# The 31-tap depthwise convolution of a streaming-encoder trunk: six channel tiles as plain fp32 matmuls on row quarters of TensorE, in place of four tiles as split fp32r on row halves and one on full rows

## The reference

```python
def causal_depthwise_conv(x, w):          # w: 31 taps by 1024 channels
    k, c = w.shape
    return lax.conv_general_dilated(
        x, w[:, None, :].astype(x.dtype), window_strides=(1,), padding=[(k - 1, 0)],
        dimension_numbers=("NWC", "WIO", "NWC"), feature_group_count=c)

def mixer_conformer_conv(x, w_pw1, b_pw1, w_dw, b_dw, ln_g, ln_b, w_pw2):
    h = x @ w_pw1 + b_pw1
    a, g = jnp.split(h, 2, axis=-1)
    h = a * jax.nn.sigmoid(g)
    h = causal_depthwise_conv(h, w_dw) + b_dw
    h = jax.nn.silu(layer_norm(h, ln_g, ln_b))
    return h @ w_pw2
```

## Time and profile before

| | before |
|---|---|
| median of three runs | 2538.86 us (2538.58 to 2539.81) |
| the profiled execution's own time | 2539.48 us |
| span of its trace | 2537.7 us |
| TensorE matmul busy | 2515.6 us, 99% |
| VectorE (DVE) busy | 1955.7 us, 77% |
| ScalarE (ACT) busy | 1201.1 us, 47% |
| DMA | mean 95 GB/s |
| granted TensorE clock | 90% or more of full speed in each of 40 slices |

### The profile page before, as it was taken

How to read it: one execution, slowest core, us unless ns; L and a number is a source line. 1 busy time by engine, 2 the same in 40 slices (tenths; PEclk the granted TensorE clock), 3 DMA queues, 4 the chain that set the end, 5 groups by cost and what they waited for, 6 DMA issues and landing times. The chain is left out here.

```text
span 2537.7 us, 41266 instructions
## 1 busy us (share of the span) xinstructions
PE 2515.6 (99%) x17241; PEld 2312.0 (91%) x17241; DVE 1955.7 (77%) x2571; ACT 1201.1 (47%) x1960; POOL 1.4 (0%) x10
## 2 busy tenths in 40 slices
PE   9999999999999999999999999999999999999999
PEld 7899999889888899998898899998898999999888
DVE  6989999578454679995784479996677979999576
ACT  6766444436233254443362254444356766444335
POOL 0000000000000000000000000000000000000000
PEclk9999999999999999999999999999999999999999
DMA  5203333324232233333233224333222203333322
GB/s 157 74 11 100 108 108 101 108 83 133 92 99 84 84 92 101 108 105 104 83 100 100 92 66 125 101 108 108 92 92 93 67 26 100 101 109 101 108 82 77
DMA packets 267054, 240.10 MB, mean 95 GB/s; under 512 B 14908, under 2 KB 212852, under 8 KB 266740
## 3 DMA queue, kind: packets, MB, share of 16 engines
q1 hardware_dynamic: 266292, 236.94, 30.1%
q10 hardware_dynamic: 576, 0.52, 0.1%
HBM read 233.21 MB, written 2.10 MB: 93 GB/s over the span
## 5 line engine op out<-in xcount | busy, mean ns | idle before, releaser
L1786 DVE TENSOR_TENSOR w_lo<-raw,w_hi 128x1024 fp32r<-128x1024 f32 x287 | 345.2, 1221 | 265.1 <-ACT w_hi L1309 264.6
L1309 ACT CAST w_hi<-raw 128x1024 fp32r<-128x1024 f32 x287 | 294.9, 1046 | 375.2 <-DMA raw<-in_ffn_w_down_dram 106.4
L879 PE MATMUL psum<-h_hi,w_lo 128*128 128x512 f32 x872 | 341.4, 392 | 0.0
L881 PE MATMUL psum<-h_hi,w_hi 128*128 128x512 f32 x872 | 339.3, 389 | 0.0
L880 PE MATMUL psum<-h_lo,w_hi 128*128 128x512 f32 x856 | 333.2, 389 | 0.0
L1024 PE MATMUL psum<-a_hi,w_lo 128*128 128x256 f32 x1088 | 280.0, 285 | 5.2 <-DVE w_lo L1786 3.6
L1024 PE MATMUL psum<-a_hi,w_hi 128*128 128x256 f32 x1088 | 276.6, 283 | 0.0
L1190 PE MATMUL psum<-h_hi,w_hi 128*128 128x256 f32 x768 | 217.3, 283 | 0.0
L1191 PE MATMUL psum<-h_hi,w_hi 128*128 128x256 f32 x768 | 217.3, 283 | 0.0
L1024 PEld LDWEIGHTS psum<-a_hi,w_lo 128*128 128x128 f32 x1088 | 208.6, 192 | 7.4 <-issue 3.7
L1321 ACT CAST w_hi<-w_hi_f 128x1024 fp32r<-128x1024 f32 x96 | 101.0, 1052 | 230.1 <-DVE w_hi_f L1814 230.1
(11 more groups left out here) (362 smaller groups left out, 6490.4 us busy)
## 6 DMA issues: line engine op xcount, KB each, us to landing
raw<-in_ffn_w_gate_dram SPq DMA_DIRECT2D x176, 256.0 KB, 3.0
raw<-in_ffn_w_up_dram SPq DMA_DIRECT2D x176, 256.0 KB, 3.4
raw<-in_ffn_w_down_dram SPq DMA_DIRECT2D x176, 256.0 KB, 3.2
raw<-in_a_w_pw_dram SPq DMA_DIRECT2D x94, 256.0 KB, 3.1
raw<-in_ple_w_gate_dram SPq DMA_DIRECT2D x64, 256.0 KB, 3.3
raw<-in_b_w_in_dram SPq DMA_DIRECT2D x64, 256.0 KB, 3.0
raw<-in_c_w_in_dram SPq DMA_DIRECT2D x48, 256.0 KB, 2.9
raw<-in_b_w_out_dram SPq DMA_DIRECT2D x32, 256.0 KB, 3.1
```

What stands on the lines that cost most here:

```text
L879: pe.matmul(bank(grp.g, j), st_lo, mv_hi, start=(k == 0), stop=False, skip_group_check=by_tiles(grp))
L881: done = pe.matmul(bank(grp.g, j), st_hi, mv_hi, start=False, stop=(ku == last and a == UK - 1), skip_group_check=by_tiles(grp))
L1309: act.copy(hi_u[u % RING], raw_u[u % RING]).then_inc(hi_ready, 1)
L1786: dve.tensor_tensor(lo_u[u % RING], raw_u[u % RING], hi_u[u % RING].bitcast(F32), ALU.subtract)\
```

## The change

All of tiles 2 to 7 go to TensorE as plain fp32 matmuls, without a split into parts; DVE keeps tiles 0 and 1.

- Tiles 2 to 6 are done over four output phases (`quad_tap`): the input is laid out by token modulo 4, a stationary block has 32 rows (channels) by 128 columns (32 channels by 4 phases), and a matmul has 128 columns. The four groups of channels r = 0 to 3 use a quarter of the array's rows each and write four banks. A tile has 34 steps, 136 matmuls.
- Tile 7 is done over two phases in two halves of tokens (`pair_tap`): blocks of 64 rows, 128 columns, two matmuls a step, 32 steps for each half, 128 matmuls.
- `SEGMENTS` lists the seven pieces of TensorE's work; piece i writes the half of PSUM of i's parity, and waits for the copies out of piece i - 2.
- The copies out of PSUM shift partitions themselves, with 16 small copies for each of the tiles 2 to 6 (32 partitions by 128) and 4 for each half of tile 7 (64 by 128). `move(s, i, high)` does the copies of two banks (or one), on ACT or on DVE. ACT has all of pieces 0 and 1, the low ones of 2, the high ones of 3 and all of 4; DVE has the rest. The DMAs, `phase_place`, `phase_add` and `conv_evict` go.
- Blocks are made on DVE, one multiplication for all 31 taps (`make_blocks`), and ACT only copies the input into phase order (`conv_by_phase`). The split parts, `taps_lo`, the diagonals and some 500 ACTIVATEs go.
- The mean (`centre`) is made within piece 3 and kept from two matmuls of 256 columns; piece 4 waits for its copy.
- In `conv_norm`, ACT loads the table for sqrt before it copies out the first half of tile 7, and copies out the second half before it applies the norm to the first.

```diff
-PHASED = ((4, 0), (5, 0), (3, K_SHARED), (6, 0))
+QUADS = (2, 3, 4, 5, 6, 7)
+A_BLOCKS = 5
+SEGMENTS = ((0, None), (1, None), (2, None), (3, None), (4, None), (5, 0), (5, 1))
+CENTRE_IN, CENTRE_AT = 3, 14
+STATS_AT = 12
...
-            def phase_tap(s, n, e):
-
-                at = e % 2 * (CW // 2) + e // 2
-                for w, x in ((0, 1), (1, 0), (0, 0)):
-                    for r in range(2):
-                        moving = conv_split(n, x)[r * TILE_ROWS:(r + 1) * TILE_ROWS, at:at + HALF]
-                        last = pe.matmul(phase_bank(s, n, r)[:, 0:HALF], block_pair(n, e, w, r), moving,
-                                         start=(e == PHASED[n][1] and (w, x) == (0, 1)),
-                                         stop=(e == TAPS_A and (w, x) == (0, 0)))
-                return last
+            def quad_tap(s, i, e):
+
+                n = SEGMENTS[i][0]
+                for r in range(PHASES):
+                    moving = rows(conv_phases(n), r)[:, e % PHASES, e // PHASES:e // PHASES + SEGMENT]
+                    block = rows(tap_blocks(n), r)[:, e * ROWS:e * ROWS + P]
+                    last = pe.matmul(segment_bank(s, i, r), block, moving, start=(e == 0), stop=(e == STEPS - 1))
+                return last
 
-            def last_tap(k, o, h):
-
-                x_hi, x_lo = (conv_split(len(PHASED), part)[:, h * HALF + k:h * HALF + k + HALF] for part in range(2))
-                pe.matmul(o, diag(k, 0), x_lo, start=(k == 0), stop=False)
-                pe.matmul(o, diag(k, 1), x_hi, start=False, stop=False)
-                return pe.matmul(o, diag(k, 0), x_hi, start=False, stop=(k == TAPS_PE - 1))
+            def pair_tap(s, i, e):
+
+                n, at = SEGMENTS[i][0], e // 2 + SEGMENT * SEGMENTS[i][1]
+                for r in range(2):
+                    own = slice(r * PAIR_ROWS, (r + 1) * PAIR_ROWS)
+                    last = pe.matmul(segment_bank(s, i, r), tap_blocks(n)[own, e * PAIR_ROWS:e * PAIR_ROWS + P],
+                                     conv_phases(n)[own, e % 2, at:at + SEGMENT], start=(e == 0), stop=(e == PAIR_STEPS - 1))
+                return last
...
+                for i, (n, h) in enumerate(SEGMENTS):
+                    if i < 2:
+                        take_half(s.taps_g + i)
                     else:
+                        pe.wait_ge(moved_high, moved(s, i - 2))
+                        pe.wait_ge(moved_low, moved(s, i - 2))
+                    if i == CENTRE_IN + 1:
+                        pe.wait_ge(centre_saved, c + 1)
+                    pe.wait_ge(conv_phased, len(QUADS) * c + n + 1)
+                    pe.wait_ge(blocks_made, len(QUADS) * c + n + 1)
+                    for e in range(STEPS if h is None else PAIR_STEPS):
+                        last = quad_tap(s, i, e) if h is None else pair_tap(s, i, e)
+                        if i == CENTRE_IN and e == CENTRE_AT:
                             centre(s)
+                        if i == LAST and e == STATS_AT:
+                            conv_stats(s, 0)
                     last.then_inc(taps_done, 1)
...
+            def move(s, i, high):
+
+                act.wait_ge(taps_done, moved(s, i))
+                for y, out_of in moves(s, i, high):
+                    last = act.copy(y, out_of)
+                last.then_inc(moved_high if high else moved_low, 1)
...
+                        conv_by_phase(s, 4)
+                        conv_by_phase(s, 5)
                         split_more(AHEAD)
+                        for i in range(2):
+                            move(s, i, 1)
+                            move(s, i, 0)
+                        move(s, 2, 0)
                         save_centre(s)
                         conv_squares(s)
+                        act.wait_ge(moved_high, moved(s, 2))
+                        move(s, 3, 1)
+                        conv_square(s, 4)
+                        move(s, 4, 1)
+                        act.wait_ge(moved_low, moved(s, 3))
+                        move(s, 4, 0)
+                        conv_square(s, 5)
+                        conv_square(s, 6)
                         conv_norm(s)
```

More of the change, by code:

```diff
@@ L403, in prm_taps, with moved, mean_bank, square @@
+        def moved(s, i):
+            return len(SEGMENTS) * (s.layer // 3) + i + 1
+        def mean_bank(s):
+            return bank(s.taps_g, 0, 2).rearrange("p (h s) -> p h s", h=2)[:, :, SEQ // PHASES:SEQ // PHASES + HALF]
+        def square(m):
+            return tiles(h_f32, m - TILES)
         def prm_taps(s):
@@ L769, in _ @@
                             load_x(u + 1)
-                        if s.kind == "mixer_out" and s.layer % 3 == 0 and grp.index == 1 and ku == AHEAD:
-                            for n in range(len(PHASED)):
-                                turn_phases(s, n)
                         load(u, parts_of(s, grp, ku * UK))
@@ L916, in centre @@
             def centre(s):
+                pe.wait_ge(moved_low, moved(s, CENTRE_IN - 1))
                 pe.wait_ge(ysum_ready, s.layer // 3 + 1)
-                pe.matmul(bank(s.taps_g + 1, 0), ones_r[:, :], ysum[:, :], start=True, stop=True).then_inc(centre_done, 1)
+                for h in range(2):
+                    last = pe.matmul(mean_bank(s)[:, h], ones_r[:, :], hcol(ysum, h), start=True, stop=True)
+                last.then_inc(centre_done, 1)
             def conv_stats(s, h):
+                pe.wait_ge(moved_high, moved(s, LAST - 1 + h))
                 pe.wait_ge(conv_sums, 4 * (s.layer // 3) + 2 * h + 1)
@@ new lines, in move, with centre_sum @@
+            def move(s, i, high):
+                dve.wait_ge(taps_done, moved(s, i))
+                for y, out_of in moves(s, i, high):
+                    last = dve.tensor_copy(y, out_of)
+                last.then_inc(moved_high if high else moved_low, 1)
+            def centre_sum(s):
+                own.settle()
+                wait_moved(s, 0)
+                wait_moved(s, 1)
+                for m in range(2):
+                    own.add(dve.scalar_tensor_tensor(tiles(tmp, 4 + m), conv_tile(2 + m), conv_bias(s, 2 + m), conv_tile(m),
+                                                     ALU.add, ALU.add))
@@ L1918, in place_centred, with make_blocks @@
-            def place_centred(s, n):
-                m = PHASED[n][0]
-                dve.wait_ge(phase_turned[n], 64 * (s.layer // 3 + 1))
-                dve.scalar_tensor_tensor(by_phase(tiles(h_f32, CONV_Y + m)), phased(turned(n)[1]), col("a_b_dw", s.layer // 3, m),
-                                         by_phase(mean[:, :]), ALU.add, ALU.subtract).then_inc(z_ready, 3)
+            def make_blocks(s, n):
+                edge, pattern = (PHASES - 1, rep[:, :]) if n < A_BLOCKS else (1, rep_pair)
+                width = pattern.shape[1]
+                blocks = tap_blocks(n).rearrange("p (k s) -> p k s", s=width)
+                taps = prm_taps(s).rearrange("p (k m) -> p k m", m=DT)[:, :, QUADS[n]:QUADS[n] + 1]
+                dve.wait_ge(const_ready, 7 + PHASES)
+                own.add(dve.memset(blocks[:, 0:edge], 0.0))
+                own.add(dve.memset(blocks[:, TAPS_A + edge:TAPS_A + 2 * edge], 0.0))
+                dve.tensor_tensor(blocks[:, edge:edge + TAPS_A], many(pattern, TAPS_A),
+                                  taps.broadcast_to([P, TAPS_A, width]), ALU.mult).then_inc(blocks_made, 1)
@@ L1937, in conv_sums_of @@
-                own.add(dve.tensor_tensor(both, y(0, 2), y(2, 2), ALU.add))
-                own.settle()
-                own.add(dve.tensor_tensor(both, both, y(4, 2), ALU.add))
-                place_centred(s, 3)
+                dve.tensor_tensor(three(conv_tile(0, 2), 2), three(conv_tile(0, 2), 2), many(mean[:, :], 2), ALU.subtract)\
+                   .then_inc(z_ready, 1)
+                place_centred(s, 2)
+                place_centred(s, 3)
+                wait_moved(s, 2)
+                place_centred(s, 4)
@@ L1951, in conv_sums_of @@
[L1951 to L1960 removed]
+                own.add(dve.tensor_tensor(sum_sq, tiles(tmp, 0), tiles(tmp, 1), ALU.add))
@@ L2264, in convolve @@
                             own.add(dve.scalar_tensor_tensor(y, x, w, y, ALU.mult, ALU.add))
-            def tap_alone(s, m, k, y, fresh=False):
-                x, w = conv_x[:, m, k:k + SEQ], col("a_w_dw", s.layer // 3 * TAPS_A + k, m)
-                if fresh:
-                    own.add(dve.tensor_scalar(y, x, w, None, ALU.mult))
-                else:
-                    own.add(dve.scalar_tensor_tensor(y, x, w, y, ALU.mult, ALU.add))
-            def convolve_alone(s, m, first, end):
-                sums = tiles(h_f32, CONV_Y + m), tiles(tmp, 5)
-                for k in range(first, end):
-                    own.settle(back=1)
-                    tap_alone(s, m, k, sums[(k - first) % 2], fresh=(k == first + 1))
-                own.settle()
-                own.add(dve.tensor_tensor(sums[0], sums[0], sums[1], ALU.add))
             def gated_input(s, grp):
```

459 lines of the change are left out of this document (163 added, 296 removed).

## The result

| | before | after |
|---|---|---|
| median | 2538.74 us (4 runs, 2538.58 to 2539.81) | 2525.23 us (4 runs, 2520.98 to 2526.28) |
| the profiled execution's own time, its span | 2539.48, 2537.7 us | 2524.76, 2523.0 us |

The ratio is 0.9943, with a 95% interval of 0.9926 to 0.996. On a second chip the changed kernel took 2522.71 us (5 runs, 2521.27 to 2525.91) against 2539.98, 0.9933 [0.992, 0.9947]. The change makes the kernel 13.5 to 17.3 us faster; 16.4 were forecast.

A forecast was written before the change was run, and what follows sets the result against it. TensorE, busy for 99% of the span, was taken as the bound. Per layer the terms sum to 58.1 against 65.6 us, less 0.7 at L929: 8.2 saved, 16.4 for both, so 2523 us, range 2516 to 2605.

The forecast's parts named there:

- likeliest case: The forecast itself: 16.4 us saved over both layers, 2523 us, with a chance of 0.53.
- Quarters side by side: Tiles 2 to 6: four quarter-row matmuls overlap, 0.230 us a step, 170 steps, 39.1 us a layer.
- The entry: Going from full-row matmuls into the row split before the convolution: there before and stays, 0.2 us a layer.
- Tile 7: Tile 7 on row halves: 64 steps of two overlapping matmuls at 0.230 us, 14.7 us a layer.
- The statistics and the wait ahead of them: Mid tile 7: statistics 1.4 us, plus TensorE waiting 0.7 us (0 to 1.5) for the first half's sums.
- The end: After the convolution: ACT copies out the second half before the norm; TensorE's wait of 0.78 us becomes 1.4.
- L929: TensorE's wait of 0.7 us there goes, its sums no longer standing behind the conversion of a full tile.
- Copies: Copies out of PSUM: below 0.30 us each, sixteen at most 4.8 us, hidden under a 7.8 us piece; zero cost.
- Rival A: Matmuls waiting for their rows hold back later ones: quarter step 0.46 us, 2601 us in all; chance 0.26.
- Rival B: TensorE's instruction rate limits quarter steps: at 0.045 us a record, 0.36 us a step, 2567 us; chance 0.11.
- Rival C: Scattering copies cost 0.5 us, sixteen 8.0 against a piece of 7.8, so TensorE waits: 2533 us; chance 0.08.
- D: Rival: quarters don't run side by side at all, 0.90 us a step, 2750 us; chance 0.02.

The follow-up runs named there:

- experiment 1: Changed kernel with piece 4's 8 low copies moved from ACT to DVE: 2519.66 us, 0.9923 of before; on the second chip 2520.92 against 2522.71 us.
- experiment 2: On top of experiment 1, DVE also does all four copies of the last half of tile 7: 2519.87 us.
- experiment 4: Changed kernel with 2, 9 or 34 steps of one quarter issued in a row: 2523.23, 2918.5, 3000.61 us; quarters of 128, 124, 120, 116 columns: 2520.62 us.
- experiment 6: Changed kernel with ACT making each of its copies of pieces 0 and 1 twice: 2533.83 us.
- experiment 5: Changed kernel, 64 instead of 128 moving columns in tiles 2 to 6: 2525.7 us; another mixing four step sizes (fewer quarters, moving or block columns): 2552.76 us.
- experiment 3: On top of experiment 1, ACT makes the first two `a_hi` before its last copies and DVE copies earlier: 2519.66 us, 0.9922 of before.

## Why the prediction was right

The forecast held: 2523 for 2525.2 and 2522.7, in its likeliest case.

- *Quarters side by side.* 0.230 us a step were taken, 0.2234 measured. 170 steps make 38.0, the mean 0.65, the first four and the step to the halves 0.1 each, and small stalls 1.0: 39.8, for 39.9 in the sum (39.1 + 0.2 + 0.5 + 0.1). The stalls were not in the sum; the upper value of the step paid for them. In layer 3 they are 1.3 us longer, which is all of the difference between 59.2 and 57.9. The entry of 0.45 us (99.47 to 99.92) lies ahead of the first start, and the sum should not have had it.
- *Tile 7.* 64 steps at 0.2235 are 14.3, for 14.7.
- *The statistics and the wait ahead of them.* 2.0 us from the last pair before them to the first after, less the pair's own 0.11, for 1.4 + 0.7. The wait is 0.84 us measured, 0.7 forecast, by the chain that the prediction gave: copies of piece 4, two squares, table load, copies, placing, square, sum. That piece 4's copies are in that chain, experiment 1 shows. The size was luck in part. The prediction had ACT ready some 1 us after the first half of tile 7 and 2 more for the rest, against 3.0 of matmuls, which leaves no wait; the 0.7 was taken from a range. ACT was ready 2.3 us after it (149.2 against 146.9), and the rest took 1.7.
- *The end.* 1.36 for 1.4. The prediction's reason, two copies ahead of the norm on ACT, was half of it: the bank being emptied sets an end of its own, 0.28 us earlier in the changed kernel (experiment 2).
- *L929.* Its wait is gone. The one of 1.0 for `a_lo` stays, at 0.9.
- *Copies.* The step that says "a copy of 32x128 lies below 0.30" is wrong: 0.39 to 0.40 on ACT and on DVE. The nearest rows were of small tiles with neighbouring elements; a stride of 16 bytes on the output costs half as much again. Between the pieces it did no harm, 6.3 us being under 7.7. Behind piece 4 it did: 6.3 us and not 4.8 make ACT 1.5 us later for the table load, and without these the wait of 0.84 at L900 would not be there (an estimate from these rows; experiment 1, which takes eight of these copies off ACT, has no wait there). The prediction put piece 4's copies at zero.
- *Rival A* is refuted by the fours and by experiment 4: a step takes 0.223, not 0.46. The Trainium skill ("TensorE: Matmul & The Clock Gate", the section on the mechanism of row and column tiling) has matmuls start in program order; here, by the likely reading of experiment 4, records on busy rows were passed by those of the other three quarters, and, if the program reaches TensorE in the order in which it is written, the measurement decides against the page for this case. Beyond about four records a quarter the order does hold them back (2918.5 and 3000.61 us), and there the page's picture is the nearer one.
- *Rival B* is refuted by piece 0 with blocks of 64 columns: 0.0147 us a record. *Rival C*'s copies of 0.5 didn't come; experiment 6 shows that its mechanism is real from 0.48 us a copy on (7.7 / 16). *D* fell with the fours.

The sum had 16.4 us, the two profiled executions differ by 14.7. Of the 1.7, the clock after the waits of layer 0 took 1.7 (experiment 1) and the longer stalls of layer 3 1.3; 0.2 in layer 0 and some 0.4 in the rest of layer 3's convolution went the other way, and 0.7 between the stretches I have not traced. The clock and the stalls are the terms that the prediction did not have; in layer 0 the step taken too long made up for the stalls, which is luck too.

## What to carry to other kernels

Small fp32 products on quarters of TensorE's rows ran side by side at full pace here, even though each is two records on the same rows, with two and with four records in a row on the same quarter, and hardly overlapped with 18; interleave quarters in the program. Before cutting moving columns, look at the block's columns: with 128 of these a record takes 0.112 us at 64 moving columns too. Where an engine copies out behind TensorE, price the copy from a row with the same output stride (0.39 us here, not 0.26), and count the copies that stand ahead of a table load or a norm by themselves. Where a wait has two ends (a norm and a bank), move work away from both or neither.

## What the hardware showed that was not expected

- Records of other quarters start ahead of some that wait for busy rows, as far as about four records of a quarter, by the likely reading: full pace with 2 and 4 records in a row, three or four overlapped at each change with 18 and 68 (experiment 4).
- A record with 128 block columns takes 0.112 us at 64 and at 128 moving columns; with 64 and 64 a record comes every 0.0147 us on four quarters (experiment 5).
- With one quarter of the rows at work the granted clock fell to 0.50, 1.2 GHz, after 3.1 us and stayed there (0.51 over 270 us in the order with 34 steps); with two quarters at work it stayed at 0.50, to which it had fallen before. With four quarters, and with two halves, it was 1.00 (experiments 4, 5).
- Waits of 1.4 and 0.9 us close to each other are followed by a stretch at 1.2 GHz in some executions of the same kernel and not in others, which costs 1.7 us each time (experiment 1); waits of 1.0 and 0.6 were too, in one of two layers (experiment 3).
- A 32x128 copy out of PSUM takes 0.26 us to neighbouring elements and 0.39 to every fourth (experiment 6).
